# One place for side work between the two passes of a weight unit, and a new timetable for a state-space scan

## The reference

```python
def trunk_layer(x, p, attend, conv_buf, ssm_h0):
    xn = rmsnorm(x, p['g_mix_norm'])
    z = xn @ p['w_in']                                   # 2048 -> 5120
    q, k, v, u, h, gb, gc = jnp.split(z, SPLITS, axis=-1)
    o_att = attend(q, k, v)                              # prompt: 3 dilated windows; samples: against the cache
    y_ssm, h_re, h_im = ssm_mixer(u, p, ssm_h0)          # 64 complex states per group, a scan over time
    y_conv, conv_state = conv_mixer(h, gb, gc, p['conv_w'], conv_buf)
    mixed = concat([rmsnorm(o_att, g1), rmsnorm(y_ssm, g2), rmsnorm(y_conv, g3)])
    x = x + mixed @ p['w_out']
    xn = rmsnorm(x, p['g_ffn_norm'])
    return x + (silu(xn @ p['w_gate']) * (xn @ p['w_up'])) @ p['w_down']   # width 5632
y = rmsnorm(x, g_final)
```

## Time and profile before

| | |
|---|---|
| three runs | 1517.65, 1517.92, 1519.74 us (median 1517.92) |
| profiled execution | 1516.64 us, its span 1514.8 us |
| granted TensorE clock | 0.997 of full speed over the span |
| busy share of the span | PE 99%, DVE 54%, ACT 39%, POOL 14% |
| chain that ended last | PE 93%, DVE 5%, ACT 1%, issue 1% |
| HBM traffic | 289.3 MB read, 195 GB/s over the span |

### The profile page before, as it was taken

How to read it: one execution, slowest core, us unless ns; L and a number is a source line. 1 busy time by engine, 2 the same in 40 slices (tenths; PEclk the granted TensorE clock), 3 DMA queues, 4 the chain that set the end, 5 groups by cost and what they waited for, 6 DMA issues and landing times.

```text
span 1514.8 us, 27139 instructions
## 1 busy us (share of the span) xinstructions
PE 1494.9 (99%) x11083; PEld 1412.8 (93%) x11083; DVE 823.5 (54%) x1073; ACT 583.9 (39%) x792; POOL 217.9 (14%) x316
## 2 busy tenths in 40 slices
PE   9999999999999999999999999999999999999997
PEld 8998777777778999999999999999999999999997
DVE  6659998863567577445444444445444433343334
ACT  6334333346555344433333333333333333234332
POOL 7864443400530000000000000000000000000100
PEclk9999999999999999999999999999999999999998
DMA  7647799999887444444444444444444444444442
GB/s 257 196 154 242 259 358 378 341 367 366 331 317 278 154 142 151 153 145 148 151 152 145 147 151 152 147 146 150 152 148 145 151 153 149 146 151 153 145 152 107
DMA packets 83138, 296.59 MB, mean 196 GB/s; under 512 B 9968, under 2 KB 11120, under 8 KB 82672
## 3 DMA queue, kind: packets, MB, share of 16 engines
q1 hardware_dynamic: 82912, 295.16, 57.6%
q10 hardware_dynamic: 144, 0.26, 0.1%
HBM read 289.31 MB, written 5.43 MB: 195 GB/s over the span
## 4 chain that ended last, share of the span: by engine, by line
PE 93%; DVE 5%; ACT 1%; issue 1%; DMA 0%; SPq 0%; DVEq 0%; ACTq 0%
PE ps L1974 20%; PE ps L1972 20%; PE ps L1973 20%; PE ps L1824 8%; PE ps L1826 4%; PE ps L1862 3%; PE ps L1864 2%; PE ps L1863 2%; PE ps L1636 2%; PE ps L1665 2%; DVE wlo L977 1%; PE ps L1925 1%; PE ps L1923 1%; PE ps L1924 1%; PE ps L1738 1%
## 5 line engine op out<-in xcount | busy, mean ns | idle before, releaser
L1278 DVE TENSOR_TENSOR wlo<-raw,whi 128x1024 fp32r<-128x1024 f32 x264 | 325.2, 1232 | 519.9 <-ACT whi L858 519.8
L858 ACT ACTIVATE whi<-raw 128x1024 fp32r<-128x1024 f32 x264 | 279.9, 1060 | 606.2 <-PE ps L1974 601.7
L1974 PE MATMUL ps<-xh,wlo 128*128 128x320 f32 x1400 | 432.6, 309 | 0.0
L1972 PE MATMUL ps<-xh,whi 128*128 128x320 f32 x1400 | 432.6, 309 | 0.0
L1973 PE MATMUL ps<-xl,whi 128*128 128x320 f32 x1400 | 432.6, 309 | 0.0
L1973 PEld LDWEIGHTS ps<-xl,whi 128*128 128x128 f32 x1400 | 262.8, 188 | 0.0
L1972 PEld LDWEIGHTS ps<-xh,whi 128*128 128x128 f32 x1400 | 262.8, 188 | 0.0
L1974 PEld LDWEIGHTS ps<-xh,wlo 128*128 128x128 f32 x1400 | 262.8, 188 | 0.0
L1972 PE MATMUL ps<-hh,whi 128*128 128x320 f32 x696 | 215.1, 309 | 0.0
L1973 PE MATMUL ps<-hl,whi 128*128 128x320 f32 x696 | 215.1, 309 | 0.0
L1974 PE MATMUL ps<-hh,wlo 128*128 128x320 f32 x696 | 215.1, 309 | 0.0
(11 more groups left out here) (330 smaller groups left out, 1819.7 us busy)
## 6 DMA issues: line engine op xcount, KB each, us to landing
raw<-in_w_gu SPq DMA_DIRECT2D x176, 512.0 KB, 3.5
raw<-in_w_dn SPq DMA_DIRECT2D x88, 512.0 KB, 3.5
raw<-in_w_in SPq DMA_DIRECT2D x79, 512.0 KB, 5.2
kv<-in_ck SPq DMA_DIRECT2D x76, 512.0 KB, 6.3
kv<-in_cv SPq DMA_DIRECT2D x64, 512.0 KB, 7.2
raw<-in_w_out SPq DMA_DIRECT2D x32, 512.0 KB, 3.6
raw<-in_cv SPq DMA_DIRECT2D x16, 512.0 KB, 7.9
out_kv<-z SPq DMA_DIRECT2D x2, 1280.0 KB, 12.7
```

The lines of the kernel that those rows point to most:

```text
L858: act.activation(whi[:, j % SPL, :], raw[:, j % RAW, :], ACT.Copy).then_inc(S["w_hi"], 1)
L1278: v.tensor_tensor(wlo[:, j % SPL, :], raw[:, j % RAW, :], whi[:, j % SPL, :].bitcast(F32), ALU.subtract) \
L1972: t_.matmul(out, whi[:, slot, w], ah[:, k, :], start=(k == 0), stop=False)
L1974: last = t_.matmul(out, wlo[:, slot, w], ah[:, k, :], start=False, stop=(k == 2 * units - 1))
```

## The change

1. **Timetable of the scan.** The 80 parts are spread over slots 24 to 64 by weights: 0 in slots with s%8 = 6, 10 up to slot 35, 12 up to 42, 19 from 43 on. Before, 18 parts lay evenly in slots 24 to 36 and 62 in 37 to 64. By the end of slot 42, 27 parts are done where it was 32; slots 43 to 63 then have three parts each in 14 slots and none in 46, 54 and 62.
2. **One place.** In units with 0 < s%8 < 7 and s < 66, `middle(s)` and `end(s)` stand together between the passes, at the end of the 16 matmuls with `whi`. In most slots keys (`scores`) and values come first and `middle` last; in slots with turns (`states_first`) `middle` comes first and keys last. `fills` and the load order of keys and values follow.
3. **Start.** Each pair of x is loaded ahead of the weight unit it goes with; both tiles of pair 1 are made ahead of `high(1)` and `low(1)`.
4. **Small moves.** Squares of the attention one slot earlier; evictions 2 and 3 of slot 79 behind its masks; the convolution's `normed` as a whole in slot 85; pieces 1, 3 and 5 of y issued by ACT.

```diff
-SCAN0, SCAN1, SCAN_END, SCAN_FIRST = 24, 37, 65, 18
+SCAN0, SCAN1, SCAN2, SCAN_END = 24, 36, 43, 65
+        SCAN_TIME = [0 if s % U_IN == U_IN - 2 else 10 if s < SCAN1 else 12 if s < SCAN2 else 19 for s in range(SCAN_END)]
         def scan_slot(i, part):
-            s = even_slot(5 * i + part)
-            return s + (s % U_IN == U_IN - 2 and 5 * i + part > 0 and even_slot(5 * i + part - 1) == s)
+            start = sum(SCAN_TIME[SCAN0:]) * (5 * i + part) // (5 * ST)
+            return next(s for s in range(SCAN0, SCAN_END) if sum(SCAN_TIME[SCAN0:s + 1]) > start)
+        def one_place(s):
+            return s < PROMPT0 and 0 < s % U_IN < U_IN - 1
+        def states_first(s):
+            turns = [b for b in range(DEC_BATCH) if s - START_OF[b] in (TURN, TURN + 1)]
+            return bool(turns) or any(s - t in (0, 1) for t in LATE_SLOTS)
...
             for j in range(1, U_IN):
+                sy.dma_start(x1[:, 2 * j:2 * j + 2, :], a["xt"][:, 2 * j:2 * j + 2, :]).then_inc(S[f"x_in{j}"], 16)
                 if j < RAW:
                     unit(j)
-                sy.dma_start(x1[:, 2 * j:2 * j + 2, :], a["xt"][:, 2 * j:2 * j + 2, :]).then_inc(S[f"x_in{j}"], 16)
...
-            gained_high(V_MIX, 2, 1)
+            x_high(1)
             act.wait_ge(S["warmed"], 1)
             high(1)
-            gained_high(V_MIX, 3, 1)
...
-                if s in (ATT0 + 3, ATT0 + 5):
+                if s in (ATT0 + 3, ATT0 + 4):
...
+            for n in (1, 3, 5):
+                first, tiles = Y_DVE[n]
+                act.wait_ge(S["y_ready"], n + 1)
+                act.dma_start(o["y"][:, first:first + tiles, :], yout[:, first:first + tiles, :]).then_inc(S["stored"], 16)
...
-            gained_low(V_MIX, 0, 2, 1)
+            gained_low(V_MIX, 0, 1, 2)
             low(1)
-            gained_low(V_MIX, 0, 3, 1)
...
-                if is_last(s) and s >= 2 * U_IN - 1:
+                if is_last(s) and s >= 2 * U_IN - 1 and s != N_IN - 1:
...
+                if s == N_IN - 1:
+                    evict(s, 2)
+                    evict(s, 3)
                 low(s + 2)
...
-                    normed(ZH, V_OUT, rstd, range(0, 2))
                 if s == SUM_CONV + 2:
-                    normed(ZH, V_OUT, rstd, range(2, NC))
+                    normed(ZH, V_OUT, rstd)
...
-                if s == ATT0 + 6:
+                if s == ATT0 + 5:
...
+            def keys(s):
                 for b in batches(s, TURN + 1):
                     turn_probabilities(b, 2)
                 for step in range(KN):
                     for b in batches(s, step):
                         scores(b, step)
+            def end(s):
+                if one_place(s) and states_first(s):
+                    middle(s)
+                for b in batches(s, OUTPUT):
+                    if b >= LATE:
+                        turn_output(b)
+                if not states_first(s):
+                    keys(s)
                 for j in range(0, KEY_TILES, 2):
                     for b in batches(s, VALUES + j // 2):
                         values(b, j)
                         values(b, j + 1)
+                if states_first(s):
+                    keys(s)
+                elif one_place(s):
+                    middle(s)
...
                     if src is wlo:
+                        if one_place(u):
+                            end(u)
                         pe.wait_ge(S["w_lo"], RAW + u + 1)
...
-                        if src is whi and n == 2:
+                        if src is whi and n == 2 and not one_place(u):
                             middle(u)
...
                     inner_unit(u, j, b0)
-                    end(u)
+                    if not one_place(u):
+                        end(u)
```

More of the change, by code:

```diff
@@ L429, in fills @@
                     end.append((4, ("turn", b)))
+            keys = []
             for b in batches(s, TURN + 1):
-                end.append((7, ("pt", b, 2)))
+                keys.append((7, ("pt", b, 2)))
             for step in range(KN):
                 for b in batches(s, step):
-                    end.append((6, ("score", b, step)))
+                    keys.append((6, ("score", b, step)))
+            if not states_first(s):
+                end += keys
             for b in batches(s, VALUES):
                 end.append((4, ("av", b)))
+            if states_first(s):
+                end += keys
+            elif one_place(s):
+                end += middle
+                middle = []
             for b in batches(s, TURN):
@@ L457, in build @@
             here = [("k", b, i, half) for i in range(KN) for b in batches(s, i) for half in range(2)]
-            here += [("v", b, j, 0) for b in range(DEC_BATCH) for j in range(KEY_TILES) if START_OF[b] + VALUES + j // 2 == s]
+            vals = [("v", b, j, 0) for b in range(DEC_BATCH) for j in range(KEY_TILES) if START_OF[b] + VALUES + j // 2 == s]
+            here = vals + here if states_first(s) else here + vals
             KV_ORDER += here
@@ L599, in _ @@
             weights("dn")
-            for name, pieces, n in (("y_ready", Y_DVE, 0), ("y_ready", Y_DVE, 1), ("y_ready", Y_DVE, 2), ("y_ready", Y_DVE, 3), ("y_first", Y_POOL, 0),
-                                    ("y_ready", Y_DVE, 4), ("y_ready", Y_DVE, 5), ("y_first", Y_POOL, 1), ("y_ready", Y_DVE, 6)):
+            for name, pieces, n in (("y_ready", Y_DVE, 0), ("y_ready", Y_DVE, 2), ("y_first", Y_POOL, 0), ("y_ready", Y_DVE, 4), ("y_first", Y_POOL, 1),
+                                    ("y_ready", Y_DVE, 6)):
                 first, tiles = pieces[n]
@@ L741, in _ @@
                 act.activation(whi[:, 0, half], raw[:, 0, half], ACT.Copy).then_inc(S[("hi_first", "w_hi")[kk]], 1)
-            act.wait_ge(S["x_in1"], 16)
-            gained_high(V_MIX, 2, 1)
+            x_high(1)
             act.wait_ge(S["warmed"], 1)
             high(1)
-            gained_high(V_MIX, 3, 1)
             x_high(2)
@@ L800, in _ @@
                     att_high(s - ATT0)
-                if s in (ATT0 + 3, ATT0 + 5):
-                    c = (s - ATT0 - 3) // 2
+                if s in (ATT0 + 3, ATT0 + 4):
+                    c = s - ATT0 - 3
                     act.activation(sqa[:, 4 * c:4 * c + 4, 0:SEQ], z[:, ZQ + 4 * c:ZQ + 4 * c + 4, 0:SEQ], ACT.Square).then_inc(S["sq_ready"], 1)
@@ L1098, in prompt_norms, with normed @@
                         v.tensor_scalar(sp[:, e, lo:hi], sp[:, e, lo:hi], pmax[:, 3, n:n + 1], None, ALU.mult).then_inc(S["pp_norm"], 1)
-            def normed(first, gain, rstd, tiles=range(NC)):
-                for c in tiles:
+            def normed(first, gain, rstd):
+                for c in range(NC):
                     v.scalar_tensor_tensor(out=z[:, first + c, :], in0=z[:, first + c, :], scalar=vec[:, gain + c:gain + c + 1], in1=rstd[:],
```

4 lines of the change are left out of this document (removed).

## The result

The changed kernel takes 1532.07 us (median of 4, 1531.18 to 1536.71) where the kernel before, in the same series, takes 1518.57: a ratio of 1.0097, 95% interval 1.0084 to 1.011. It is slower by 13.5 us; 1523 had been forecast, with 1514 to 1529 as the range. The profiled execution took 1531.29 us with a span of 1529.5, 14.7 more than before.

A forecast was written before the change was run, and what follows sets the result against it. TensorE, busy 99% of the span, was taken as the bound: gains of 9.1 us against new waits of 12.5 and 2.0 give +5.4 on 1516.64, so 1522.0; with 1.3 for the median, forecast 1523 us, range 1514 to 1529.

The forecast's parts named there:

- The four waits: Slots 44, 45, 50, 52: project waits for its own place's scores' mask, 2.9, 3.0, 2.6 and 4.0, sum 12.5 us.
- Start: Start of the kernel: earlier pair 1 of x shortens TensorE's waits, gain 1.6 us, bounds 0.9 and 2.1.
- Small moves: Later edits: slot 79's masks 0.8, squares one slot earlier 1.2, `normed` 0.3, outputs from ACT 0; gain 2.3 us.
- Old waits: Waits in slots 44, 49, 41 and 31 to 32 shrink by 1.3, 0.8, 0.5 and 1.0: 3.6 us gained.
- Joined places: Slots 24 to 65: eight side places fewer at 0.19 us each, gain 1.6 us.
- The rule that speaks for half of the gain: A tiling mode change drains TensorE; one of two switches stays, so joined places save 0.8 us rather than 1.6.
- The rest of the joined places have smaller ones: Smaller waits in the other joined places, slots 58, 60, 39, 54 and 63: about 2.0 us in all (1 to 3).
- contention: Parts 0 and 1 in slots 43 to 52 fall on POOL's tables: about 19 us of waits; 0.12 with late loads.
- Late keys and values: Scores and values reach TensorE before their DMA, 200 to 260 us: +3.6, 1527 us; 0.12 together with contention.
- The masks in time: Project hardly waits for masks in the joined places: -6.1 us, 1511.8 us; chance 0.13.

The follow-up runs named there:

- E2: Changed kernel with the project ahead of the scores in the joined place, in slots 36 to 65 that have a project: 1523.16 us, 1.003.
- E5: Changed kernel with 16, 16 and 18 extra matmuls ahead of the project in slots 44, 50 and 52: 1533.95 us, 1.0095.
- E4: Changed kernel with the old places (`one_place` false), so new timetable, start and small moves only: 1512.18 us, 0.9963.
- E1: Kernel before with the start and the small moves alone, old timetable and old places: 1513.61 us, 0.9969.
- E8: Changed kernel with only `end` between the passes, project and `read_out` in their old place: 1525.48 us, 1.0046.
- E6: Changed kernel with DVE's scan parts of slots 43, 44, 49 and 51 behind the next slot's masks: 1525.02 us, 1.0039.
- E11: E5 with 16 more extra matmuls ahead of the project of slot 45: 1529.89 us, 1.0076.
- E9: E4 with ACT's `ptk` copies right behind `high`, ahead of the next state's decay: 1511.5 us, 0.9949.
- E3: Changed kernel with the old timetable of the scan: 1528.15 us, 1.0065.
- E7: Changed kernel with the project behind the whole unit where it shares a place with scores: 1528.18 us, 1.0068.
- E10: E8 with ACT's `ptk` copies of a slot ahead of its `high` and decay: 1521.87 us, 1.0021.

## Why the prediction was wrong

*The direction was right, and the mechanism in part.* Slower was forecast at 0.68, with the project behind its own place's scores as the cause. That wait is there and has the forecast's size: 2.9 expected in slot 44, 2.78 measured as idle time (the loop and the arrival without a wait were each 0.1 to 0.2 us longer than forecast). But taking the project out of its way (E2) gives back 8.1 of 18.3 us. Slot 50 was put at 2.6 and took 2.91, slot 52 at 4.0 and took 3.31. Slot 45 was put at 3.0 and took 1.46: ahead of it the matmuls ran at half clock and lost 1.5 us, while DVE did not. In E5, where slot 44 kept the clock, it waited 2.78. The four waits come to 10.5 for 12.5.

*The small sizes.* Start 1.6 forecast, 1.3 measured. Small moves 2.3, measured 2.3 (0.8, 0.3, 1.2). Old waits in slots 24 to 65: 3.6 forecast; the 1.3 and 0.8 went, 1.5 became 0.5, but 1.1 of waiting stays, in slot 31, where `low(31)` now comes behind two scan parts (E4 has it too; E1, with the old timetable, has the eviction's). Joined places: 1.6 forecast; nothing of it is seen. The changed kernel's waits (15.5 us, less 4.6 of before, the slow project's 0.8 among them) and its clock (6.2) make 17.1 of the 18.3, so places saved nothing within an error of a microsecond or so. No run joined places without moving them, so what takes the gain back stays open. The rule that speaks for half of the gain isn't refuted, and isn't shown.

*The step that failed* is the sentence "The rest of the joined places have smaller ones", with about 2.0 us in all. Only slots with a project were asked about. But the change moves every `end` of an inner unit ahead of eight matmuls, and E8 shows that this by itself costs 12.0 us: each side place comes 1.2 us sooner than its helpers' order allows. In the changed kernel the mask waits hide much of it: TensorE is late anyway, so the waits for `ptk` are only 0.9 in all, and the waits besides the four and slot 31's come to 3.8 us. That would be why my four waits came out near their size, and why taking them away (E2, E6) gives back 8 and 7 us and not the 17 of waits and clock: the masks and the moved `end` look like two prices of which the larger is paid. So 2.0 was too low by 1.8 in the changed kernel's own list, and far lower than what the place costs by itself: E2, whose masks are in time, still loses 10.1.

*The term that was missing* is the clock, 6.2 us by the pitches. The profile before had a row that asked for it: TensorE kept full clock through waits of up to 1.5 us, and there was no row with a wait of 3 us. A forecast of four such waits left the range that the trace had seen. With 10.5 + 3.8 of waits, 6.2 for the clock, and gains of 1.3 + 2.3 + 3.5, the sum of measured terms is +13.4 of 14.7. So of the 9.3 us between the forecast for the profiled execution (1522.0) and its time, the clock is 6.2, the smaller waits 1.8, the joined places 1.6, start and old waits 0.4, less 2.0 for the four waits that were put too high; 1.3 is in no term. That the four waits' -2.0 and the smaller waits' +1.8 nearly cancel is luck.

The rivals: contention (1528 and over) came nearest in size, but not by POOL: parts 0 and 1 ahead of slot 45's mask took 2.74 us, as when POOL was still, and that wait was the shortest of the four. Late keys and values: TensorE has no wait for a DMA in the list after. The masks in time: no.

On the clock the Trainium skill, "TensorE: Matmul & The Clock Gate", section "HAM oscillation — how this bites in real kernels", takes the extra time as the time at the lower clock times one half. For 13.7 us that is an estimate of 6.8; by the pitches here it is 6.2, as a pitch falls from 0.267 to 0.147 and not to half, and E11 against E5 measures 4.5 for 10.2 us.

## What to carry to other kernels

A side place is fed by engines whose queues are anchored on the main work's semaphore; when it is moved ahead of that semaphore, price for every place who produces what it needs, and behind which waiting instruction that producer stands. Two waits on one path are not added: the longer one is paid, so removing it uncovers the other, and an experiment that moves only one thing (E8) tells more than one that mends the visible wait. When a forecast adds waits longer than any in the profile, add the clock's price, here at most 1.5 us for each stretch of 3.4, and less where a later wait takes it back. Look for the cheap part of a change by itself: here the timetable and the small moves alone are 0.4% faster than the kernel before by the medians (E4), and 0.5% with one reordering on ACT (E9); by the profiled executions 4.2 and 5.2 us, 0.3% each.

## What the runs showed that I had not expected

**Where the clock falls.** All stretches at half clock ahead of the end are 3.41 or 6.83 us long. They begin between 0.5 us before and 2 us behind the end of a wait. But a wait doesn't decide alone: 2.74 us in slot 41 of E3 and 3.15 in slot 54 of E8 had none, while 1.41 in E7 did, and those at 298 us in E2, 299 in E6 and 309 in E5 stand behind a wait of 0.4 us. In the profiled executions of before, E1, E4 and E9, whose longest waits in these slots are 1.49, 1.47, 1.38 and 1.15 us, there was none. What decides is left open.

**The clock differs between executions of one kernel.** That the profile before has no such stretch doesn't mean that the kernel never has. Over 38 executions of it in the series of the experiments, time and granted clock (the mean over the span) go together:

| granted clock | executions | us |
|---|---|---|
| 0.997 (as profiled) | 8 | 1516.71 to 1517.89, one 1519.85 |
| 0.996 | 11 | 1517.43 to 1518.66 |
| 0.995 | 16 | 1518.78 to 1519.84 |
| 0.994 | 3 | 1520.49 to 1520.96 |

So half of them, at 0.995 and less, had lost clock that the profile doesn't show, and most of the scatter of this kernel goes with it; where in the program it was lost isn't on record. E1 and E4 were at 0.996 to 0.997 in every execution. About 1.8 us of what they gain by the medians is the clock of the kernel before: E1 gains 4.5 by the medians and 2.8 in the profiled executions, E4 6.0 and 4.2.

**The last microseconds.** From the start of the last matmul on the weights to the span's end it takes 14.3 us before, in the changed kernel and in E11, but 15.1 in E1, E2, E4, E5 and E7 to E10, with the same instructions. The clock falls there too, while TensorE waits for the final norm or just behind that wait: 5.2 to 5.3 us behind that matmul in the first three, 2.7 to 3.8 in the others (E3 and E6 lie in line: 4.5 and 14.6, 2.4 and 15.2), so that more of the last matmuls run at half clock: the twelve that turn the norm's factors span 1.74 us in the changed kernel and 2.83 in E4. The table by stretch for the changed kernel and for E9, from the fall of the clock on:

```profile
1520.00:1529.50 9.50, 0.93 (x7) 0.74 (x6) 4.54 (x7) 0.44 (x1) 3.03 (x2) 0.52 0.73 276
```

```profile
1498.00:1509.70 11.70, 2.82 (x12) 2.63 (x12) 5.03 (x10) 1.03 (x3) 3.03 (x2) 0.52 0.59 224
```

So of what E1, E4 and E9 gained earlier 0.8 us is given back there. Why the fall comes sooner in them was not tried.
